# Reordering small pieces at three joints of a decoder-layer kernel: the second weight unit, the entry to the feed-forward part, and both layer norms

## The reference

```
sh1,sc1,g1,sh2,sc2,g2 = c @ w_ada + b_ada                   # 2048 x 12288
u   = x * (1 + sc1) + sh1
z_pool, x_conv, B, C, gate_pool, gate_conv = u @ w_in       # 2048 x 8192
y_p = (windowed means of z_pool - z_pool), grouped map, @ w_pool_up
y_c = (B * dwconv3(C * x_conv)) @ w_conv_up
mix = (sigmoid(gate_pool) * y_p + sigmoid(gate_conv) * y_c) @ w_o
x   = LN1(alpha * x + g1 * mix)
u2  = x * (1 + sc2) + sh2
x   = LN2(alpha * x + g2 * (relu(u2 @ w_ff1 + b_ff1)^2 @ w_ff2 + b_ff2))   # 2048 x 8192, 8192 x 2048
```

## Time and profile before

| | |
|---|---|
| median of three runs | 1462.76 us |
| the profiled execution's own time | 1462.99 us |
| its span, first to last instruction | 1461.0 us |
| TensorE (PE) matmuls busy | 1445.8 us, 99% |
| VectorE busy | 854.3 us, 58% |
| ScalarE busy | 534.9 us, 37% |
| GpSimd busy | 101.1 us, 7% |
| TensorE's granted clock, mean | 0.999 of full |
| HBM traffic | 340 MB read, 235 GB/s over the span |

### The profile page before, as it was taken

How to read it: one execution, slowest core, us unless ns; L and a number is a source line. 1 busy time by engine, 2 the same in 40 slices (tenths; PEclk the granted TensorE clock), 3 DMA queues, 4 the chain that set the end, 5 groups by cost and what they waited for, 6 DMA issues and landing times.

```text
span 1461.0 us, 28172 instructions
## 1 busy us (share of the span) xinstructions
PE 1445.8 (99%) x11851; PEld 1363.4 (93%) x11851; DVE 854.3 (58%) x1055; ACT 534.9 (37%) x392; POOL 101.1 (7%) x99
## 2 busy tenths in 40 slices
PE   7999999999999999999999999999999999999998
PEld 6899888898898899997899999999999999999997
DVE  4677565565688655449745445554545555454557
ACT  3333223223326323234634333343334433343335
POOL 1000000000350000000050000000000000000800
PEclk9999999999999999999999999999999999999999
DMA  9987888888896796995755555555555555555541
GB/s 317 388 293 263 296 313 303 294 321 297 297 337 233 271 329 245 327 332 202 276 181 178 174 183 189 173 175 188 184 172 180 186 180 173 183 189 174 174 171 60
DMA packets 174286, 343.36 MB, mean 235 GB/s; under 512 B 6036, under 2 KB 16312, under 8 KB 174201
## 3 DMA queue, kind: packets, MB, share of 16 engines
q1 hardware_dynamic: 172562, 340.36, 67.2%
q0 software_dynamic: 752, 1.31, 0.3%
q10 hardware_dynamic: 912, 0.85, 0.2%
HBM read 340.19 MB, written 2.79 MB: 235 GB/s over the span
## 4 chain that ended last, share of the span: by engine, by line
PE 96%; DVE 2%; SPq 1%; DMA 1%; issue 0%; DVEq 0%; ACT 0%
PE main L1556 30%; PE main L1557 29%; PE main L1558 29%; PE ps_ada L1590 5%; DMA raw<-in_w_in 1%; SPq L386 1%; DVE w_lo L981 0%; PE ps_adat L1689 0%; DVE G L1415 0%; DVE U L1447 0%; DVE G L1409 0%; ACT w_hi L653 0%; DVE G L1404 0%; PE main L1951 0%; PE ps_adat L1691 0%
## 5 line engine op out<-in xcount | busy, mean ns | idle before, releaser
L653 ACT ACTIVATE w_hi<-raw 128x2048 fp32r<-128x2048 f32 (+1 forms) x227 | 429.7, 1894 | 880.0 <-PE main L1558 861.1
L981 DVE TENSOR_TENSOR w_lo<-raw,w_hi 128x2048 fp32r<-128x2048 f32 (+1 forms) x212 | 482.1, 2274 | 453.8 <-ACT w_hi L653 453.3
L1556 PE MATMUL main<-U,w_hi 128*128 128x264 f32 (+1 forms) x2320 | 662.4, 286 | 1.4 <-DVE PB L1143 0.6
L1558 PE MATMUL main<-U,w_lo 128*128 128x264 f32 (+1 forms) x2320 | 658.7, 284 | 0.0
L1557 PE MATMUL main<-U,w_hi 128*128 128x264 f32 (+1 forms) x2192 | 620.1, 283 | 0.0
L1556 PEld LDWEIGHTS main<-U,w_hi 128*128 128x128 f32 x2320 | 436.0, 188 | 35.3 <-issue 31.2
L1558 PEld LDWEIGHTS main<-U,w_lo 128*128 128x128 f32 x2320 | 435.4, 188 | 0.0
L1557 PEld LDWEIGHTS main<-U,w_hi 128*128 128x128 f32 x2192 | 412.0, 188 | 0.0
L1556 PE MATMUL main<-H,w_hi 128*128 128x264 f32 x1280 | 364.9, 285 | 0.0
L1558 PE MATMUL main<-H,w_lo 128*128 128x264 f32 x1280 | 362.2, 283 | 0.0
L1557 PE MATMUL main<-H,w_hi 128*128 128x264 f32 x1152 | 327.3, 284 | 0.0
(11 more groups left out here) (258 smaller groups left out, 589.9 us busy)
## 6 DMA issues: line engine op xcount, KB each, us to landing
raw<-in_w_ff SPq DMA_DIRECT2D x128, 1024.0 KB, 5.1
ada_raw<-in_w_ada SPq DMA_DIRECT2D x80, 1024.0 KB, 6.9
raw<-in_w_in SPq DMA_DIRECT2D x63, 1024.0 KB, 10.0
raw<-in_w_o SPq DMA_DIRECT2D x16, 1024.0 KB, 10.3
raw<-in_w_pool_up SPq DMA_DIRECT2D x8, 1024.0 KB, 9.7
raw<-in_w_conv_up SPq DMA_DIRECT2D x8, 1024.0 KB, 9.2
PB<-in_w_ada SPq DMA_DIRECT2D x6, 1024.0 KB, 12.4
PB<-in_w_ada SPq DMA_DIRECT2D x8, 512.0 KB, 9.2
```

Of the source, the lines that this page charges most:

```text
L653: nc.scalar.activation(w_hi[:, s % HL, 0:size], raw[:, s, 0:size], ACT.Copy).then_inc(hi_ready, 1)
L981: tt(w_lo[:, s % HL, 0:size], raw[:, s, 0:size], w_hi[:, s % HL, 0:size].bitcast(F32), ALU.subtract).then_inc(unit_split, 1)
L1556: mm(out, wh, x_hi, start=start, stop=False)
L1558: return mm(out, wl, x_hi, start=False, stop=stop)
```

## The change

Six edits, in three places.

1. **Second weight unit.** ACT rounds the unit n = 1 in two instructions of 128x1024 in place of one of 128x2048, and DVE's first two low pieces of it wait for the first of them.
2. **Gap loads.** Loads 5 and 6 go into X (tiles 0 to 7, 8 to 15) and wait for `x_moved`, which `minus_guess(3)` raises; 7 goes into PB 16 to 23. SP issues 5 and 6 before the fourth load of the first FF block. Load 11 takes load 5's slot in X. `GAP_NEXT` becomes (6, 2, 2), so that eight of the twelve stand ahead of FF.
3. **Second FF unit.** Its low part is made in four pieces of 512 columns (`ff_piece`): one where `lo_part` was, three behind `lo_u2` of tiles 6 and 7; TensorE waits for the pieces one by one.
4. **Layer norm.** DVE adds one pair of squares (tiles 12 and 13); tiles 14 and 15 go to TensorE each by itself. So TensorE has three `last_moment` matmuls in place of two, and the first of them stands in front of `full_mean`.
5. **End.** The product `stat_t` of the mean's rows moves from ACT to POOL.
6. **End.** The reciprocal `std_rec` on DVE moves behind the second `stat_r`.

```diff
@@
 C_AT = (GROUP - 1) * SEQS
 GAP_ADA = 12
-GAP_HELD = 5
-GAP_FIRST, GAP_NEXT = 2, (5, 3, 2)
+GAP_HELD, GAP_MOVED = 5, 7
+GAP_FIRST, GAP_NEXT = 2, (6, 2, 2)
 U2_ALL = KC + 3
@@
         z_ready, z_scaled, proj_ready = sem("z_ready"), sem("z_scaled"), sem("proj_ready")
         cols_gathered = sem("cols_gathered")
+        x_moved = sem("x_moved")
+        ff_pieces = sem("ff_pieces")
         yp_out, yp_hi, up_pieces = sem("yp_out"), sem("yp_hi"), sem("up_pieces")
@@
         w_half = a["w_in"][0].rearrange("(h c p) n -> h p c n", c=2, p=P)
         gap_slot = [ada_u[:, 0], ada_u[:, 1], eight_tiles(Uf, 0), eight_tiles(Uf, 16),
-                    eight_tiles(PB, 8), eight_tiles(PB, 16), eight_tiles(PB, 24), eight_tiles(PB, 0)]
+                    eight_tiles(PB, 8), eight_tiles(X, 0), eight_tiles(X, 8), eight_tiles(PB, 16)]
         gap_slot += [gap_slot[k] for k in (0, 1, 4, 5)]
@@
...
                     sp.wait_ge(part_done, done(U_WO - 1))
+                elif k < GAP_MOVED:
+                    sp.wait_ge(x_moved, 1)
                 else:
@@
...
             load_wo(3)
-            for j in range(4):
+            for j in range(3):
                 load_ff1(0, 0, j)
-            for k in range(GAP_HELD, GAP_ADA - 2):
+            for k in range(GAP_HELD, GAP_MOVED):
+                load_gap(k)
+            load_ff1(0, 0, 3)
+            for k in range(GAP_MOVED, GAP_ADA - 2):
                 load_gap(k)
@@
                 pool.drain()
             r.then_inc(rows_ready, 1)
+            pool.wait_ge(off_ready, 1)
+            g_ts(stat_t[g_part], off[g_part, 0:PROMPT], stat_l[g_part], None, ALU.mult).then_inc(off_parts, 1)
+
             g_s = G[:, 0:NT, PROMPT:TOK]
@@
                 act.wait_ge(u_shifted, t + 1)
                 nc.scalar.copy(U[:, t, :], Uf[:, KC + t, :]).then_inc(u_hi_ready, 1)
-            def half_of(w, h):
-                return w[:, 0, :].rearrange("p (c n) -> p c n", c=2)[:, :, h * UC:(h + 1) * UC]
+            def half_of(w, h, s=0):
+                return w[:, s, :].rearrange("p (c n) -> p c n", c=2)[:, :, h * UC:(h + 1) * UC]
             copy_x(range(X_FIRST))
@@
...
             for n in range(N_IN):
-                hi_part((n + 1) % RAW, (n + 1) // RAW, n + 1)
+                if n == 0:
+                    act.wait_ge(raw_landed[1], landed(0))
+                    act.wait_ge(part_done, split_slot_free(1))
+                    nc.scalar.activation(half_of(w_hi, 0, 1), half_of(raw, 0, 1), ACT.Copy).then_inc(half_hi, 1)
+                    nc.scalar.activation(half_of(w_hi, 1, 1), half_of(raw, 1, 1), ACT.Copy).then_inc(hi_ready, 1)
+                else:
+                    hi_part((n + 1) % RAW, (n + 1) // RAW, n + 1)
                 if n == 1:
@@
...
                     act.wait_ge(mask_ready, 1)
-                    nc.scalar.copy(stat_hi[g_part], off[g_part, 0:PROMPT])
-                    nc.scalar.activation(stat_t[g_part], off[g_part, 0:PROMPT], ACT.Identity,
-                                         scale=stat_l[g_part]).then_inc(off_parts, 1)
+                    nc.scalar.copy(stat_hi[g_part], off[g_part, 0:PROMPT]).then_inc(off_parts, 1)
                 act.drain()
@@
                 if n == 0 and p < 2:
                     dve.wait_ge(half_hi, p + 1)
+                elif n == 1 and p < 2:
+                    dve.wait_ge(half_hi, 3)
                 else:
@@
...
                     minus_guess(2).then_inc(ln_d, 1)
-                    minus_guess(3)
+                    minus_guess(3).then_inc(x_moved, 1)
                     dve.wait_ge(ln_sq, LN_D * l + 2)
@@
             def norm(l):
                 sq = G[:, 2 * NT - MT:2 * NT, :]
-                for k in (0, 2):
-                    dve.wait_ge(ln_sq, LN_D * l + 3 + k + 2)
-                    tt(sq[:, k, :], sq[:, k, :], sq[:, k + 1, :], ALU.add).then_inc(ln_sums, 1)
+                dve.wait_ge(ln_sq, LN_D * l + 3 + 2)
+                tt(sq[:, 0, :], sq[:, 0, :], sq[:, 1, :], ALU.add).then_inc(ln_sums, 1)
                 dve.wait_ge(ln_mean, 2 * l + 2)
@@
...
                           ALU.subtract)
+
+            def ff_piece(m):
+                if m == 0:
+                    dve.wait_ge(hi_ready, U_FF + 2)
+                lo, r, hi = (w[:, 1, :].rearrange("p (c n) -> p c n", c=KC)[:, :, m * P:(m + 1) * P]
+                             for w in (w_lo, raw, w_hi))
+                tt(lo, r, hi.bitcast(F32), ALU.subtract).then_inc(ff_pieces, 1)
             norm(0)
@@
...
             normalise(KC + 2, 2, prompt).then_inc(ln_norm, 1)
-            lo_part(1, U_FF + 1)
+            ff_piece(0)
             lo_u2(KC + 1, KC, 2)
             lo_u2(KC + 2, KC + 2, 2).then_inc(u2_ready, 1)
+            for m in range(1, MT):
+                ff_piece(m)
+            dve.drain().then_inc(unit_split, 1)
             less_off(8, KC, prompt)
@@
             norm(1)
             dve.wait_ge(stat_zero, 1)
-            dve.wait_ge(off_parts, 1)
+            dve.wait_ge(off_parts, 2)
             stt(stat_r[g_part], stat_hi[g_part].bitcast(F32), stat_d[g_part], stat_t[g_part], ALU.mult, ALU.add)
...
             cp(stat_hi[b_part], rstd[b_part, 0:PROMPT])
-            nc.vector.reciprocal(std_rec, rstd[:, PROMPT:TOK]).then_inc(std_inv, 1)
             dve.drain()
...
                 ALU.mult, ALU.add).then_inc(stat_rows, 1)
+            nc.vector.reciprocal(std_rec, rstd[:, PROMPT:TOK]).then_inc(std_inv, 1)
             dve.wait_ge(col_psum, 1)
@@
             def pe_early_moment(l):
-                pe.wait_ge(ln_sums, 3 * l + 1)
+                pe.wait_ge(ln_sums, 2 * l + 1)
                 mm(ps_b[:, 0:TOK], ones, G[:, NT, :], start=True, stop=False)
@@
             def last_moment(l, k):
-                pe.wait_ge(ln_sums, 3 * l + 2 + k)
-                r = mm(ps_b[:, 0:TOK], ones, G[:, 2 * NT - 4 + 2 * k, :], start=False, stop=k == 1)
+                if k == 0:
+                    pe.wait_ge(ln_sq, LN_D * l + 3 + 3)
+                    mm(ps_b[:, 0:TOK], ones, G[:, 2 * NT - 2, :], start=False, stop=False)
                 if k == 1:
-                    r.then_inc(ln_moment, 1)
+                    pe.wait_ge(ln_sums, 2 * l + 2)
+                    mm(ps_b[:, 0:TOK], ones, G[:, 2 * NT - 4, :], start=False, stop=False)
+                if k == 2:
+                    pe.wait_ge(ln_sq, LN_D * l + 3 + 4)
+                    mm(ps_b[:, 0:TOK], ones, G[:, 2 * NT - 1, :], start=False, stop=True).then_inc(ln_moment, 1)
             def norm(l):
                 last_mean(l)
+                last_moment(l, 0)
                 full_mean(l)
-                last_moment(l, 0)
                 last_moment(l, 1)
+                last_moment(l, 2)
             def gap_ada(first, count):
@@
...
                     pe.wait_ge(u2_ready, KC + j)
-                    unit(j, q * 32 + i * 4 + U_FF + j, q * 32 + i * 4 + T_FF, (U, 8 * j), (U, 8 * j + KC), False, j == 3)
+                    unit(j, q * 32 + i * 4 + U_FF + j, q * 32 + i * 4 + T_FF, (U, 8 * j), (U, 8 * j + KC), False, j == 3,
+                         pieces=ff_pieces if gap and j == 1 else None)
             def ff2_block(q, i, early={}):
@@
                    start=False, stop=True).then_inc(y_psum, 1)
             last_mean(1)
+            last_moment(1, 0)
             pe.wait_ge(y_tiles, NT - MT)
...
             full_mean(1)
-            last_moment(1, 0)
             last_moment(1, 1)
+            last_moment(1, 2)
             for k in range(BANKS):
```

## The result

The changed kernel took **1464.91 us** (median of 22 runs, 1464.16 to 1466.59), the kernel before, on the same chip, 1463.24 us (22 runs, 1462.47 to 1464.49). The ratio is 1.0012, 95% interval [1.0007, 1.0018]: slower by 1.7 us, about one part in 900. By the bound of the prediction (0.2%) this is no change; but the forecast was 1463.5 and its range ended at 1464.5, so the time is 1.4 us above the one and 0.4 us above the other. The profiled execution took 1464.88 us, close to its median, with a span of 1462.9 us at a mean granted clock of 0.998. Before it was 1462.99 and 1461.0. So the spans differ by 1.9 us.

A forecast was written before the change was run, and what follows sets the result against it. TensorE, busy 99% of the span, was taken as the bound, paced near FF by the norm's chain. -0.80 + 1.45 + 0.13 = +0.78 us on 1462.99 gave 1463.8, a median of 1463.5 us; range 1462.0 to 1464.5.

The forecast's parts named there:

- the first term: Second weight unit: rounding in two halves lets TensorE start it without its wait, gaining the whole 0.80 us (-0.80).
- fits by 0.1: Third weight unit: landing at 30.48, it is ready at 33.8 us, just before TensorE asks at 33.9.
- the first step does nothing: Rival at the second weight unit: the third unit's landing takes back the 0.80 us; 1464.3 us, chance 0.11.
- The second unit itself: Near 28 us: first piece and bank copy come 0.87 us sooner, and no 0.9 us distance between matmuls remains.
- The norm's order: Norm behind w_o: the extra squares matmul ahead of `full_mean` delays the mean's copy and FF's start by 0.42 us.
- The gap loads: Before FF: six units fit, TensorE idles 0.47 us till 694.42; readiness for the second FF unit at 702.4 goes unused.
- The late transfer: Rival before FF: load 7 takes 15.0 us to land and holds FF till 700.2; 1467.2 us, chance 0.03.
- The pieces: Second FF unit: three pieces delay the queue behind them by 2.35 us; third FF unit +1.45 us, including the norm's 0.42.
- The two rivals in which they cost nothing: At FF: pieces pay, 1462.0 to 1462.4 us, chance 0.15; only the norm's order costs, 1462.5 us, chance 0.13.
- The end: Last norm: the extra matmul pushes the transposes by 0.13 us; `stat_t` on POOL costs 0, `std_rec` is off the path.
- the dearer pieces: Third FF unit: upper bound of the pieces' term, +2.35 us in place of +1.45, if there is no slack.

The follow-up runs named there:

- e9: Kernel before with the second weight unit rounded in two instructions and POOL's two state loads held back until that unit landed; 1463.95 us, ratio 1.0004.
- e6: Changed kernel with two FF pieces ahead of the low part of tiles 4 and 5, one before that of tiles 6 and 7, one behind; 1463.60 us.
- e7: Changed kernel with its layer norm edit undone (two sums on DVE, two moment matmuls behind the full mean); 1464.05 us, ratio 1.0009.
- e11: Repeat of e1 (kernel before with only the second weight unit rounded in two instructions), on the chip of e9; 1462.57 us, ratio 0.9995.
- e1: Kernel before with the first edit alone, the second weight unit rounded in two instructions; 1462.96 us, ratio 0.9997.
- e8: Kernel before with two-part second-unit rounding, gap-load edit, FF pieces spread around low parts, tiles 4 and 5 normalised earlier; 1462.57 us, ratio 0.9995.
- e10: Repeat of e8, the same kernel, on the chip of e9; 1462.62 us, ratio 0.9994.
- e4: Kernel before with the gap loads edit alone (loads 5 and 6 into X, order 6, 2, 2); 1462.91 us, ratio 0.9999.
- e2: Kernel before with the layer norm edit alone (one sum less on DVE, three `last_moment` matmuls), in both norms; 1464.23 us, ratio 1.0007.
- e3: Kernel before with the pieces edit alone (second FF unit's low part in pieces, three behind tiles 6 and 7); 1464.70 us, ratio 1.0011.
- e5: Kernel before with the two end edits alone (`stat_t` on POOL, `std_rec` moved last); 1463.18 us, ratio 0.9999.

## Why the prediction was wrong

**The step that failed is the first term, "the third unit lands at 30.48 whatever happens", and so the -0.80, of which 0.01 came.** What it says of the chain from the landing to TensorE was right. In each of the seven traces with the edit (e9, with its other wait, left out) the third unit starts at the later of two times: 11.75 us behind the first unit, which is TensorE without a wait, or 3.4 us behind the start of ACT's rounding (1.91 us of rounding, a piece, a copy). After: 31.46 + 3.4 = 34.86, measured 34.86. e6: 30.71 + 3.4 = 34.11, measured 34.11. e7: 34.53, measured 34.53. e11: 34.70, measured 34.71. In e1, e8 and e10 the first unit rules (e8: 22.97 + 11.75 = 34.72, measured 34.72).

What was wrong is that 30.48 is no constant. It was read from one execution, and it is the second earliest of twelve starts of this rounding: they run from 30.11 to 31.46 us, e9 left out (the landings themselves from 30.1 to 31.4). The edit is not what made it late in after: the load was issued at 15.00 us there and at 14.96 before, 10 us before the first edited instruction, and the starts without the edit (30.48 to 31.21) and with it (30.11 to 31.46) overlap. The prediction itself said "fits by 0.1".

Nor is there always a wait to remove. Without the edit, the third unit starts 9.32 us behind the start of the second unit's rounding, which is the same 3.4 and a unit without a wait, 5.93 (before: 25.54 + 9.32 = 34.86, measured 34.87; e4: 25.46 + 9.32 = 34.78, measured 34.76) or, again, 11.75 behind the first unit. In e2 and e3 the first unit started at 24.39 and 23.96, and the second followed at 5.95 and 5.92 with no edit at all. (e5 fits neither, 35.34 us against 34.65: its first unit ran partly at half the clock, see the last section.) An estimate by these two rules, from each trace's own landings, gives what the edit is worth in it: after 0.28, e6 0.49, e8 0.24, e7 0.11, and 0 in e1, e10 and e11. In the execution that the prediction was made from it is 34.87 less 33.96 (22.21 + 11.75), 0.91, so there the term would have come out in full. **Of the executions that the rules cover, that one was the kindest to the change.** These are estimates for one execution of each kernel. The 22 runs agree: with -0.80 beside the measured +1.52 and +0.19 the change would be 0.9 us slower, and the interval of the ratio, 1.0 to 2.6 us slower, just leaves that out. The rival "the first step does nothing" (1464.3, chance 0.11) was the case that came.

**The second unit itself** went as said: the copy behind the first piece 0.87 us sooner against the landing, no distance near 28 us.

**The norm's order** was right: forecast +0.42, e2 +0.38 at FF's third unit, e7 0.41. `full_mean` is two records later, and the mean's copy at 687.67 in place of 687.23.

**The gap loads** were right: no wait of TensorE for a load in after, FF held by DVE's first tile (0.64 us idle in front of it, about 0.5 forecast), a gap group less in front of the second unit and an idle time of 0.94 us instead. The late transfer did not come.

**The pieces** were right to 0.1 us: +1.45 forecast with the norm's part, +1.52 measured. The two rivals in which they cost nothing are refuted by e3 and e6.

**The end** was right for TensorE's order (+0.13 forecast, +0.12 in e2). For `stat_t` on POOL the prediction took 0 because TensorE would not ask before 1451.5; the estimate of the instruction was 0.8 to 1.2 us, and it took 1.21. The whole chain behind it (0.39 us of waiting on DVE, then two factors) ends just after TensorE asks: +0.06, also in e5. DVE's first factor takes 0.59 us in after and in e5, where a POOL instruction had begun 0.14 and 0.13 us earlier, and 0.47 in before, where POOL's began later. The row of 1.21 us has DVE's squaring of the mean, with two inputs in SBUF, inside it (1450.80). The rule of the Trainium skill, GPSIMD Engine Reference, section Specifications, is that such DVE instructions contend with POOL for its SBUF interfaces. The trace agrees in so far as the product took 1.21 us, the upper end of the estimate; no run here has this shape alone. The estimate's source, the row of 4.13 us in the earlier trace rows, was read too simply: besides the low part of 2.28 us, a DVE instruction of 0.96 us with its inputs in SBUF (1378.35 us, before) also overlaps it.

**The sum.** Forecast -0.80 + 1.45 + 0.13 = +0.78. In its place: -0.01 + 1.52 + 0.19 = +1.70 from the marks, against +1.67 between the medians of 22 runs. The spans differ by another 0.2, of which 0.10 lie behind the correction, where the granted clock falls (below), 0.06 between third unit and `last_mean(0)`, and 0.06 in the middle outside FF's entry. The range was too narrow: it held the void first step or the dearer pieces, each by itself, and nothing for the scatter of a landing. And it was centred on a median of three runs, 1462.76, where the kernel before took 1463.24 in the 22 runs beside the result: 0.48 us of the distance of 1.4 are that.

**Is there a better version?** e8 and e10 have the lowest medians against their kernels before, -0.78 and -0.90 us. Both intervals hold 1, and e11, with the second unit's edit alone, lies as low (1462.57) as e10 on the same chip. What the traces show is 0.35 us at FF, twice, and at the second unit, by the estimate above, 0.24 us in e8 and nothing in e10. So the version is probably better than before by some 0.35 us or a little more, an estimate from the marks; the timings can't show it. Against after it is 2.45 to 2.57 us sooner by the differences of medians (+1.67 for after, -0.78 and -0.90 here), and 2.06 by the marks (1.87 at FF, 0.19 at the correction).

## What to carry to other kernels

A small gain behind a transfer's landing must be reckoned against the landing's scatter, not against one row of it: here the margin was 0.1 us and the scatter 1.35. Such a term should be forecast at its mean over several executions, or at nothing. Work that is cut in pieces should be put in the holes of its engine (here between ACT's two roundings) and not in one block ahead of the next stage's queue; DVE's idle rows show where the holes are. And the longest wait in a neighbourhood need not be the one that holds it: loads that came 1.2 us sooner gave nothing, since DVE's first tile ended at the same time.

## What the runs showed of the hardware

**The start scatters by 3.4 us.** The first main matmul stands between 21.79 (e9) and 25.18 us (e10, the same kernel as e8 with 22.97), and the span of e10 is 1462.8 us where e8's is 1460.5. That is most of what separates these two executions. Part of such a difference can be made up behind it: e1 and e11, one kernel, start 1.82 us apart and are 0.87 apart at the third unit. This is why differences below 1 us were read from marks.

**TensorE's clock is not always whole at both ends.** Windows of us, with busy time of each engine, then the granted clock, DMA share and GB/s; the last microseconds of e3, then of after:

```profile
1455.00:1457.00 2.00, 2.00 (x10) 1.11 (x9) 1.82 (x3) 1.42 (x3) 0.00 (x0) 0.86 0.43 158
1457.00:1459.00 2.00, 1.92 (x6) 0.85 (x4) 0.45 (x1) 0.05 (x1) 0.00 (x0) 0.50 1.04 368
```

```profile
1455.00:1457.00 2.00, 2.00 (x13) 1.06 (x11) 1.64 (x3) 1.25 (x3) 0.12 (x1) 1.00 0.51 190
1457.00:1459.00 2.00, 1.02 (x3) 0.35 (x2) 0.75 (x1) 0.85 (x2) 0.00 (x0) 0.55 1.04 357
```

The clock goes from 1.00 (2.4 GHz) to 0.50 (1.2 GHz) while TensorE still issues, sparsely, the last transposes. In e3 it falls before 1457 us, and the last matmul comes 9.82 us behind `last_mean(1)`; in the trace of before it is 1.00 till 1457 us, and the last matmul, at 1455.62, comes at 8.95. Nothing in e3 touches that stretch, so up to 0.9 us of an execution's time go with when the clock falls. e2 and e5, where it also falls before the last matmuls, have 9.73 and 9.69. In e5 the clock is low at the start too, in the window and in the timeline of the first unit:

```profile
22.00:24.00 2.00, 2.00 (x11) 2.00 (x10) 1.70 (x4) 1.08 (x2) 0.96 (x2) 0.50 1.02 387
```

```profile
23.00 0.42 PE L1559 MATMUL main<-U,w_lo 128*128 128x264 f32 x1
23.22 0.42 PE L1557 MATMUL main<-U,w_hi 128*128 128x264 f32 x1
```

The matmuls start 0.22 us apart there and not 0.12. Before that TensorE had done the same transposes, with the same 0.36 us of idle time, as in the trace of before, where the clock was 1.00 from 20 to 26 us. What decides it was not found.
